# Two transformer blocks on one NeuronCore: both column blocks of a fresh LayerNorm's first unit in step, and a later spread of row scales

## The chip, the core and the metric

The kernel runs on one core of a Trainium2 chip. The metric is the device time of one execution in microseconds (us), from the runs' times; the profile adds one execution taken by the hardware profiler.

## What is computed

256 tokens of width 1024 go through two blocks of two layers each. In the first block every mixer and every MLP is followed by a LayerNorm of `DN_ALPHA * x + branch`; in the second each branch is `x + 0.5 * swiglu(rms_norm(x))` or a mixer. Cut to what the change touches:

```python
for i in range(DEPTH):                       # first block
    mix = attention_mixer(x, ...) if i % 2 == 0 else mamba2_bidir_mixer(x, ...)
    x = layer_norm(DN_ALPHA * x + mix, ln1_g[i], ln1_b[i])
    x = layer_norm(DN_ALPHA * x + squared_relu_mlp(x, mlp_w1[i], mlp_w2[i]), ln2_g[i], ln2_b[i])
...
def swiglu(h, w_gate, w_up, w_down):         # second block, begins with it
    return (jax.nn.silu(h @ w_gate) * (h @ w_up)) @ w_down
```

Everything is float32 in and out.

## The kernel before

The weights stream through the core in **units** of 1 MB: 1024 rows by 256 columns (eight chunks of 128 rows, two column blocks of 128), or 256 rows by 1024 columns for a down projection. A ring of three units lies in SBUF. SyncE loads a unit into `w_raw`; ScalarE casts it to the high half `w_hi` (L852, `split`); VectorE, or GpSimd for some stretches, subtracts to make the low half `w_lo` (L1383, L752) and signals `lo_ready`. TensorE takes a unit when its low half is there (`take`) and forms three products: high by high, low by high, high by low (`three`, L2078). `project_pair` (L2152 to L2156) does the same with operand halves joined into one matmul of 512 columns; its low products land in columns T to 2T of a PSUM bank and are added by ScalarE and VectorE when the bank is read. PSUM has eight banks of 512 float32 columns here: `pg` (four) and `acc` (four; they hold the running sums of the down projections).

Every engine runs its own program in the order in which the code is written; semaphores join them. There is no planner: what stands first in an engine's queue holds up what stands behind it.

**A fresh LayerNorm.** `ln` (VectorE, L1447 to L1456) makes the new `x` and its moments, ScalarE normalises the first 128 tokens (L889), VectorE the others in four parts (L1466). TensorE transposes the chunks into the `pg` banks (L2198), with a few matmuls on zeros in between (`warm`, L2310). ScalarE applies gain and bias, two chunks at a time, into `turn_buf` (L867); VectorE splits them into `op_hi` and `op_lo` (L1406, L1407 for chunks 0 and 1 one by one, L1412 and L1413 for each later pair) and signals `xt_ready`. The first unit that reads them, the fresh unit, waits at chunk 0, chunk 1 and the first chunk of each later pair:

```python
for c, k0, k1 in ((0, 0, 4), (1, 0, 4), (0, 4, 8), (1, 4, 8)) if halves else ((0, 0, 8), (1, 0, 8)):
    ...
        elif fresh and c == 0 and (k % 2 == 0 or fresh in LN_COUNT and k == 1):
            pe.wait_ge(xt_ready, TURN_BANK[fresh] + k // 2 + 1)
```

There are four such places: `ln1_0` (before the first MLP), `ln2_0` (before the SSM's input projection, through `project`), `ln1_1` (before the second MLP; behind the fresh unit TensorE computes a small product, L2664, and VectorE copies it to `rvec`, L1851, for which the first down projection waits on `rel_row`) and `ffn1_0` (the second block's first SwiGLU; the only one of the four with `halves`).

**A SwiGLU.** Unit 1 is a piece of the gate, unit 2 of the up projection, then units 3 (gate), 4 (up), 5 (down) and so on. The RMS norm is not applied to the operand; instead its row scale, one number for each token, multiplies the gate product. `spread_rstd` (TensorE, L2280) spreads the scales over all partitions into `acc` bank 1, ScalarE copies it (L987), and VectorE multiplies with it (L1516), after `gate_add`'s first step (L1512, signals `gate_taken`), which adds the low half that ScalarE copied out (L934). Behind this multiplication come, in the engines' order: ScalarE's silu (L939), ScalarE's cast of unit 4 (L852) and its copy of the up product (L945), VectorE's low half of unit 4 (L1383), and the sum of the up banks (L1521, signals `h_sum`), then the product (L1524), the hidden operand's high and low halves (L952, L1529, signals `h_ready`). TensorE waits for `gate_taken` before unit 3, for `h_sum` before unit 4, for `h_ready` before unit 5. In `ffn1_0` VectorE first finishes the LayerNorm's `x` (L1475, L1481), and ScalarE squares it for the scales (L918 to L923) and loads a function table (L1249) before it copies the gate product.

Of the kernel before, what the change touches and what calls it, by code (L numbers as in the profile page):

```python
# [11 lines left out]
ALU = mybir.AluOpType  # L12
AX = mybir.AxisListType

P = 128
T = 256
TT = T // P
D = 1024
KC = D // P
# [27 lines left out]
U = 256  # L47
# [47 lines left out]
LN_COUNT = {n: i + 1 for i, n in enumerate(LN_NAMES)}  # L95
NORM_AT = {n: sum(NORM_PARTS[:i]) for i, n in enumerate(TURNS)}
# [95 lines left out]
def two_blocks(nc, A, out):  # L192
    with ExitStack() as ctx:
# [229 lines left out]

        def oT_bank(a):

            return pg[:, 2 - 2 * a, :]

        def main_half(b):
            return pg[:, b:b + 2, 0:T]

        def low_half(b):
            return pg[:, b:b + 2, T:2 * T]
# [409 lines left out]
        def _(act):  # L842
# [88 lines left out]
            def gate_low(u_in, it=None, per_u=0):  # L931

                act.wait_ge(unit_done, at(u_in + 1, it, per_u))
                act.copy(act_pair, low_half(0)).then_inc(gate_lo, 1)  # L934
# [19 lines left out]
            def mlp(u0, h0, between=None, late=None):  # L954
                split(u0 + 2)
                hidden(h0, u0)
# [25 lines left out]
            def swiglu(u0, h0, ahead=False):  # L982
                if not ahead:
                    split(u0 + 2)
                gate_low(u0)
# [386 lines left out]
        def _(dve):  # L1372
# [137 lines left out]
            def gate_add(h, it=None, per_h=0, first=None):  # L1510
                dve.wait_ge(gate_lo, at(h - HG_FFN[0] + 1, it, per_h))
                dve.tensor_tensor(act_pair, main_half(0), act_pair, ALU.add).then_inc(gate_taken, 1)  # L1512
# [19 lines left out]
            def mlp(u0, h0, between=None):  # L1532
                split(u0 + 2)
                hidden(h0)
# [19 lines left out]
            def swiglu(u0, h0, ahead=False):  # L1554
                if not ahead:
                    split(u0 + 2)
                gate_add(h0, first=(h0 - HG_FFN[0]) // G2)
# [153 lines left out]
            for n in range(len(SSM_COLS)):  # L1711
# [29 lines left out]
                if n < CONV_UNITS:  # L1741
# [7 lines left out]
                    for k in order:  # L1749
                        for c in range(2):  # L1750
                            wc = COL["ssm_conv_w"] + 32 * k + (16 + 2 * i + c) % 32
                            t0, t1 = max(0, mid - k), T - max(0, k - mid)
                            src = pg[:, n % 4, c * T + t0 + k - mid:c * T + t1 + k - mid]
# [315 lines left out]
        def _(pe):  # L2069
# [15 lines left out]
            def feature_chunk(u, bank, c, step=U, fresh=None):  # L2085

                for k in range(KC):
                    if fresh and c == 0 and k and (k % 2 == 0 or fresh in LN_COUNT and k == 1):
                        pe.wait_ge(xt_ready, TURN_BANK[fresh] + k // 2 + 1)
# [13 lines left out]
            def project(u, bank, tokens=False, it=None, per=0, fresh=None):  # L2103
                take(u, it, per)
                if fresh in LN_COUNT:
                    pe.wait_ge(gained, TURN_BANK[fresh] + 1)
                    pe.wait_ge(half_ready, LN_COUNT[fresh])
                elif fresh:

                    pe.wait_ge(xt_ready, TURN_BANK[fresh] + 1)  # L2110
                for c in range(2):
                    o = bank[:, c * T:(c + 1) * T]
                    ins = token_tile(u, o, c, 0, U) if tokens else feature_chunk(u, o, c, fresh=fresh)
                ins.then_inc(unit_done, 1)
# [761 lines left out]
```

## Time and profile before

| | |
|---|---|
| median of 3 runs | 1729.44 us (1729.07 to 1729.72) |
| profiled execution | span 1727.7 us from its first to its last instruction; the page gives no other time for it |
| TensorE (PE) busy | 1700.7 us, 98% of the span, 9721 matmuls |
| TensorE weight loads (PEld) | 1458.1 us, beside the matmuls |
| VectorE (DVE) | 1175.8 us, 68% |
| ScalarE (ACT) | 922.0 us, 53% |
| GpSimd (POOL) | 297.4 us, 17% |
| DMA | 293.83 MB, 170 GB/s over the span |
| mean granted TensorE clock | 1.000 |

A row of a timeline gives the start of an instruction (or of a few alike), its duration, and in brackets how long its engine had been idle before it and which instruction ended that. Matmuls overlap, so the distance between two starts, not the duration, is what a matmul costs. A weight load (PEld) that starts behind a wait marks the same moment as its matmul.

### The profile page before, as it was taken

The numbers are of one execution on the slowest core, as the hardware profiler recorded it, in microseconds if no ns is written. First come the engines' busy times: TensorE is split into PE (matmuls) and PEld (weight loads), VectorE is DVE, ScalarE is ACT, GpSimd is POOL, SyncE is SP. The second block draws the span as 40 slices with busy tenths as digits, with TensorE's granted clock in tenths as the row PEclk, the third lists the DMA queues.
The fourth block names the chain that finished last, engine by engine and source line by source line (L and its number), as shares of the span: only waits on it lengthen the run. The fifth ranks groups of instructions, "written<-read, shape, count | busy, mean of one in ns | idle before, by whom it ended". The sixth has DMA issues, their size and how long they took to land.

```text
span 1727.7 us, 25216 instructions
## 1 busy us (share of the span) xinstructions
PE 1700.7 (98%) x9721; PEld 1458.1 (84%) x9721; DVE 1175.8 (68%) x1565; ACT 922.0 (53%) x1269; POOL 297.4 (17%) x162
## 2 busy tenths in 40 slices
PE   8999999999999999999999999999999999999999
PEld 8768888899888788878888978888888889878887
DVE  5887666778476875577666876666666667856665
ACT  4664444546674544465446566444554456664443
POOL 6003000675250130010000830000000006500000
PEclk9999999999999999999999999999999999999999
DMA  9425655556405575536564523665465554435652
GB/s 283 151 86 187 226 194 177 168 154 198 142 1 168 168 237 193 179 127 209 193 194 146 196 98 123 218 192 187 156 209 184 191 187 160 141 98 195 194 194 98
DMA packets 204268, 293.83 MB, mean 170 GB/s; under 512 B 6474, under 2 KB 169776, under 8 KB 204192
## 3 DMA queue, kind: packets, MB, share of 16 engines
q1 hardware_dynamic: 201072, 285.56, 50.6%
q0 software_dynamic: 2688, 6.47, 1.4%
q8 instruction: 52, 0.85, 0.2%
q10 hardware_dynamic: 432, 0.75, 0.1%
q14 instruction: 24, 0.20, 0.0%
HBM read 291.71 MB, written 1.05 MB: 169 GB/s over the span
## 4 chain that ended last, share of the span: by engine, by line
PE 89%; DVE 5%; ACT 4%; issue 1%; POOL 1%; DMA 0%; SPq 0%; ACTq 0%; DVEq 0%; POOLq 0%
PE acc L2078 30%; PE pg L2078 14%; PE pg L2152 13%; PE pg L2156 12%; PE pg L2155 6%; PE pg L2153 6%; PE acc L2616 1%; ACT w_hi L852 1%; PE pg L2603 1%; PE pg L2718 1%; ACT arena L1054 1%; PE pg L2198 1%; POOL w_lo L752 1%; ACT op L867 1%; DVE op L1421 1%
## 5 line engine op out<-in xcount | busy, mean ns | idle before, releaser
L1383 DVE TENSOR_TENSOR w_lo<-w_raw,w_hi 128x2048 fp32r<-128x2048 f32 x231 | 539.7, 2338 | 162.7 <-ACT w_hi L852 162.6
L852 ACT CAST w_hi<-w_raw 128x2048 fp32r<-128x2048 f32 x269 | 513.0, 1908 | 66.4 <-PE pg L2078 28.3
L2078 PE MATMUL acc<-w_hi,op 128*128 128x512 f32 x1600 | 517.5, 393 | 1.7 <-DVE op L2008 1.6
L2152 PE MATMUL pg<-op,w_hi 128*128 128x512 f32 x960 | 382.3, 398 | 7.0 <-DVE op L1413 1.9
L2156 PE MATMUL pg<-op,w_hi 128*128 128x512 f32 x960 | 379.7, 395 | 0.0
L2078 PEld LDWEIGHTS acc<-w_hi,op 128*128 128x128 f32 x1600 | 300.3, 188 | 66.9 <-issue 7.4
L2078 PE MATMUL acc<-w_lo,op 128*128 128x512 f32 x800 | 311.5, 389 | 0.0
L752 POOL TENSOR_TENSOR w_lo<-w_raw,w_hi 128x2048 fp32r<-128x2048 f32 x38 | 175.1, 4615 | 682.6 <-DVE w_lo L1383 630.2
L2155 PE MATMUL pg<-op,w_lo 128*128 128x256 f32 x960 | 267.6, 279 | 0.0
L2153 PE MATMUL pg<-op,w_lo 128*128 128x256 f32 x960 | 266.4, 277 | 0.0
L2078 PE MATMUL pg<-op,w_hi 128*128 128x256 f32 x1184 | 222.9, 287 | 2.9 <-DVE op L1421 1.2
L2155 PEld LDWEIGHTS pg<-op,w_lo 128*128 128x128 f32 x960 | 180.2, 188 | 44.3 <-DVE op L1407 0.9
L2153 PEld LDWEIGHTS pg<-op,w_lo 128*128 128x128 f32 x960 | 180.5, 188 | 39.7
L2152 PEld LDWEIGHTS pg<-op,w_hi 128*128 128x128 f32 x960 | 182.1, 190 | 16.9 <-issue 4.8
L2078 PEld LDWEIGHTS pg<-op,w_hi 128*128 128x128 f32 x1184 | 187.6, 192 | 7.3 <-issue 3.5
L2156 PEld LDWEIGHTS pg<-op,w_hi 128*128 128x128 f32 x960 | 179.9, 187 | 0.0
L2078 PEld LDWEIGHTS acc<-w_lo,op 128*128 128x128 f32 x800 | 150.3, 188 | 30.2
L2078 PE MATMUL pg<-op,w_lo 128*128 128x256 f32 x592 | 167.8, 283 | 0.0
L952 ACT CAST op<-h 128x512 fp32r<-128x512 f32 x76 | 47.2, 621 | 215.1 <-PE acc L2078 189.8
L1529 DVE TENSOR_TENSOR op<-h,op 128x512 fp32r<-128x512 f32 x76 | 57.0, 750 | 84.8 <-ACT op L952 84.8
L2078 PEld LDWEIGHTS pg<-op,w_lo 128*128 128x128 f32 x592 | 113.9, 192 | 0.5 <-issue 0.5
L934 ACT COPY act_buf<-pg 128x512 f32<-128x512 f32 x44 | 25.8, 586 | 115.1 <-PE pg L2156 115.0
(342 smaller groups left out, 1704.3 us busy)
## 6 DMA issues: line engine op xcount, KB each, us to landing
w_raw<-in_mlp_w SPq DMA_DIRECT2D x64, 1024.0 KB, 5.3
w_raw<-in_ffn_w_gate SPq DMA_DIRECT2D x44, 1024.0 KB, 5.3
w_raw<-in_ffn_w_up SPq DMA_DIRECT2D x44, 1024.0 KB, 5.3
w_raw<-in_ffn_w_down SPq DMA_DIRECT2D x44, 1024.0 KB, 4.8
w_raw<-in_ssm_w_in SPq DMA_DIRECT2D x24, 1024.0 KB, 5.3
w_raw<-in_w_in SPq DMA_DIRECT2D x20, 1024.0 KB, 5.1
w_raw<-in_attn_w_in SPq DMA_DIRECT2D x8, 1024.0 KB, 10.1
w_raw<-in_ssm_w_out SPq DMA_DIRECT2D x8, 1024.0 KB, 4.9
```

What stands on the lines that cost most here:

```text
L752: pool.tensor_tensor(w_lo[:, r, :], w_raw[:, r, :], w_hi[:, r, :].bitcast(F32), ALU.subtract) \
L852: act.copy(w_hi[:, u % RING, :], w_raw[:, u % RING, :]).then_inc(hi_ready, 1)
L867: ins = act.activation(op_hi[:, j, :] if bias is None else turn_buf[:, b % 2, c, :], turn_out(name, b)[:, c * T:(c + 1) * T], ACT.Identity ...
L934: act.copy(act_pair, low_half(0)).then_inc(gate_lo, 1)
L952: act.copy(op_hi[:, at_chunk:at_chunk + 2, :], h32[:, :].rearrange("p (c t) -> p c t", c=2)).then_inc(h_hi, 1)
L1383: dve.tensor_tensor(w_lo[:, s, :], w_raw[:, s, :], w_hi[:, s, :].bitcast(F32), ALU.subtract) \
L1529: dve.tensor_tensor(op_lo[:, dst, :], h32[:, :].rearrange("p (c t) -> p c t", c=2), op_hi[:, dst, :].bitcast(F32), ALU.subtract).then_inc( ...
L2078: ins = pe.matmul(psum, l, r, start=first and i == 0, stop=last and i == 2)
L2152: pe.matmul(bank, hi, joined, start=k == 0, stop=False)
L2153: pe.matmul(bank[:, 0:T], lo, op_hi[:, k, :], start=False, stop=False)
L2155: pe.matmul(bank[:, 0:T], lo, op_hi[:, k, :], start=False, stop=False)
L2156: ins = pe.matmul(bank, hi, joined, start=False, stop=k == KC - 1)
```

## The change

The fresh unit of the four LayerNorms takes the chunks in steps (0), (1), (2, 3), (4, 5), (6, 7), and each step for column block 0 and then for block 1. The waits stay where block 0 needs them. Block 1's bank can no longer be `pg` 1, which still holds transposed chunks at that time: `project_pair` writes the fresh unit to `acc` banks 2 and 3 (`FRESH`), and its readers (`hidden`, `gate_low`, `gate_add`) take it from there; in `ln2_0` block 0 stays in `pg` 0 and block 1 goes to `acc` bank 3, which the convolution reads. In `ffn1_0` the spread of the row scales moves from behind unit 2 to between the two column blocks of unit 3. Nothing is added or removed but this: the numbers and shapes of matmuls, casts and copies are the same.

```diff
+LN_STEPS = [(0, 1), (1, 2), (2, 4), (4, 6), (6, 8)]
...
+        def conv_src(n, c):
+            return acc[:, 3, 0:T] if n == 0 and c else pg[:, n % 4, c * T:(c + 1) * T]
...
+        FRESH = 4
+
+        def pair_banks(b):
+            return acc[:, 2:4, :] if b == FRESH else pg[:, b:b + 2, :]
+
         def main_half(b):
-            return pg[:, b:b + 2, 0:T]
+            return pair_banks(b)[:, :, 0:T]

         def low_half(b):
-            return pg[:, b:b + 2, T:2 * T]
+            return pair_banks(b)[:, :, T:2 * T]
...
             def mlp(u0, h0, between=None, late=None):
                 split(u0 + 2)
-                hidden(h0, u0)
+                hidden(h0, u0, b=FRESH)
...
-                gate_low(u0)
+                gate_low(u0, b=FRESH if ahead else 0)
                 act.wait_ge(rstd_spread, (h0 - HG_FFN[0]) // G2 + 1)
                 act.copy(token_rstd, acc[:, 1, 0:T]).then_inc(rb_ready, 1)
...
-                gate_add(h0, first=(h0 - HG_FFN[0]) // G2)
+                gate_add(h0, first=(h0 - HG_FFN[0]) // G2, b=FRESH if ahead else 0)
...
-                            src = pg[:, n % 4, c * T + t0 + k - mid:c * T + t1 + k - mid]
+                            src = conv_src(n, c)[:, t0 + k - mid:t1 + k - mid]
...
+            def project_fresh(u, fresh):
+
+                take(u)
+                for k0, k1 in LN_STEPS:
+                    for c in range(2):
+                        for k in range(k0, k1):
+                            if c == 0 and k == 0:
+                                pe.wait_ge(gained, TURN_BANK[fresh] + 1)
+                                pe.wait_ge(half_ready, LN_COUNT[fresh])
+                            elif c == 0 and (k == 1 or k % 2 == 0):
+                                pe.wait_ge(xt_ready, TURN_BANK[fresh] + k // 2 + 1)
+                            o = k * U + c * P
+                            ins = three(conv_src(0, c), wslice(u, o, o + P), (op_hi[:, k, :], op_lo[:, k, :]), k == 0,
+                                        k == KC - 1)
                 ins.then_inc(unit_done, 1)
...
             def project_pair(u, b, it=None, per=0, fresh=None, between=None, halves=False):
                 take(u, it, per)
-                for c, k0, k1 in ((0, 0, 4), (1, 0, 4), (0, 4, 8), (1, 4, 8)) if halves else ((0, 0, 8), (1, 0, 8)):
-                    bank = pg[:, b + c, :]
+                if fresh in LN_COUNT:
+                    order = [(c, k0, k1) for k0, k1 in LN_STEPS for c in range(2)]
+                else:
+                    order = ((0, 0, 4), (1, 0, 4), (0, 4, 8), (1, 4, 8)) if halves else ((0, 0, 8), (1, 0, 8))
+                for c, k0, k1 in order:
+                    bank = pair_banks(b)[:, c, :]
...
             def mlp(u0, h0, fresh, between=None, late=None):
-                project_pair(u0, 0, fresh=fresh)
+                project_pair(u0, FRESH, fresh=fresh)
...
             def swiglu(u0, h0, fresh, columns=None):
-                project_pair(u0, 0, fresh=fresh, halves=True,
+                project_pair(u0, FRESH if fresh in LN_COUNT else 0, fresh=fresh, halves=True,
                              between=(lambda: turn_half(fresh, 1)) if fresh in by_columns else None)
...
-                if fresh in LN_COUNT:
-                    project_pair(u0 + 1, 2)
-                    spread_rstd()
-                else:
-                    project_pair(u0 + 1, 2, between=spread_rstd)
+                late = fresh in LN_COUNT
+                project_pair(u0 + 1, 2, between=None if late else spread_rstd)

                 def group(u, h, it=None, first=False):

                     pe.wait_ge(gate_taken, at(h - HG_FFN[0], it, 1))
-                    project_pair(u, 0, it, 3)
+                    project_pair(u, 0, it, 3, between=spread_rstd if first and late else None)

                     pe.wait_ge(h_sum, at(h, it, 1))
                     project_pair(u + 1, 2, it, 3)
...
+                elif n == 0:
+                    project_fresh(u, "ln2_0")
                 else:
-                    project(u, bank, fresh="ln2_0" if n == 0 else None)
+                    project(u, bank)
```

TensorE's order in the fresh unit of `ln1_0`, before (line numbers of the kernel before; `half_ready`, `gained` and `xt_ready` are the operand's signals):

```order
L2152 MATMUL pg<-op,w_hi 128x512 [waits half_ready,gained,lo_ready]
L2153 MATMUL pg<-op,w_lo 128x256
L2155 MATMUL pg<-op,w_lo 128x256 [waits xt_ready]
L2156 MATMUL pg<-op,w_hi 128x512
L2152 MATMUL pg<-op,w_hi 128x512 [waits xt_ready]
L2153 MATMUL pg<-op,w_lo 128x256
L2155 MATMUL pg<-op,w_lo 128x256
L2156 MATMUL pg<-op,w_hi 128x512
L2152 MATMUL pg<-op,w_hi 128x512 [waits xt_ready]
L2153 MATMUL pg<-op,w_lo 128x256
```

and now (line 2173 is the old 2152, 2174 the old 2153, 2176 and 2177 the old 2155 and 2156):

```order
L2173 MATMUL acc<-op,w_hi 128x512 [waits half_ready,gained,lo_ready]
L2174 MATMUL acc<-op,w_lo 128x256
L2173 MATMUL acc<-op,w_hi 128x512
L2174 MATMUL acc<-op,w_lo 128x256
L2176 MATMUL acc<-op,w_lo 128x256 [waits xt_ready]
L2177 MATMUL acc<-op,w_hi 128x512
L2176 MATMUL acc<-op,w_lo 128x256
L2177 MATMUL acc<-op,w_hi 128x512
L2173 MATMUL acc<-op,w_hi 128x512 [waits xt_ready]
L2174 MATMUL acc<-op,w_lo 128x256
```

The first chunk's two matmuls and the second chunk's two now stand twice, once for each block, before the third chunk's wait; before, block 1 stood behind all eight chunks of block 0.

TensorE's order in `ffn1_0` from the end of unit 2, before:

```order
L2155 MATMUL pg<-op,w_lo 128x256
L2156 MATMUL pg<-op,w_hi 128x512
L2280 MATMUL acc<-ident,rstd 128x128 [waits rstd_ready]
L2280 MATMUL acc<-ident,rstd 128x128
L2152 MATMUL pg<-op,w_hi 128x512 [waits lo_ready,gate_taken]
L2153 MATMUL pg<-op,w_lo 128x256
```

now at the same place:

```order
L2174 MATMUL pg<-op,w_lo 128x256
L2176 MATMUL pg<-op,w_lo 128x256
L2177 MATMUL pg<-op,w_hi 128x512
L2173 MATMUL pg<-op,w_hi 128x512 [waits lo_ready,gate_taken]
L2174 MATMUL pg<-op,w_lo 128x256
```

and between the two blocks of unit 3 (line 2301 is the old 2280):

```order
L2176 MATMUL pg<-op,w_lo 128x256
L2177 MATMUL pg<-op,w_hi 128x512
L2301 MATMUL acc<-ident,rstd 128x128 [waits rstd_ready]
L2301 MATMUL acc<-ident,rstd 128x128
L2173 MATMUL pg<-op,w_hi 128x512
L2174 MATMUL pg<-op,w_lo 128x256
```

The spread stood ahead of the wait for `gate_taken`; it now stands sixteen matmuls behind it. On ScalarE and VectorE only the names of the banks that are read change, not the order.

## Rows read from the trace of the kernel before

**Rows 1.** The profile's page: shares of the last chain; GpSimd's subtractions.

```profile
PE 89%; DVE 5%; ACT 4%; issue 1%; POOL 1%; DMA 0%; SPq 0%; ACTq 0%; DVEq 0%; POOLq 0%
...
L752 POOL TENSOR_TENSOR w_lo<-w_raw,w_hi 128x2048 fp32r<-128x2048 f32 x38 | 175.1, 4615 | 682.6 <-DVE w_lo L1383 630.2
```

**Rows 2.** Timeline of PE, ln1_0: start us, us, instruction, [idle before <-releaser].

```profile
127.44 0.50 PE L2152 MATMUL pg<-op,w_hi 128*128 128x512 f32 x1 [0.50 <-DVE op L1413]
...
129.75 0.50 PE L2152 MATMUL pg<-op,w_hi 128*128 128x512 f32 x1
...
130.55 0.40 PE L2152 MATMUL pg<-op,w_hi 128*128 128x512 f32 x1
...
133.34 0.40 PE L2152 MATMUL pg<-op,w_hi 128*128 128x512 f32 x1
```

**Rows 3.** Timeline of all engines, ln1_0: VectorE behind the fresh unit.

```profile
129.61 4.48 DVE L1383 TENSOR_TENSOR w_lo<-w_raw,w_hi 128x2048 fp32r<-128x2048 f32 x2
...
136.26 0.69 DVE L1529 TENSOR_TENSOR op<-h,op 128x512 fp32r<-128x512 f32 x1 [0.69 <-ACT op L952]
```

**Rows 4.** Timeline of all engines, ln2_0: TensorE (PE, PEld) and VectorE.

```profile
310.71 0.39 PE L2078 MATMUL pg<-op,w_hi 128*128 128x256 f32 x1 [0.49 <-DVE op L1413]
...
312.88 2.28 DVE L1383 TENSOR_TENSOR w_lo<-w_raw,w_hi 128x2048 fp32r<-128x2048 f32 x1
313.01 0.19 PEld L2078 LDWEIGHTS pg<-op,w_hi 128*128 128x128 f32 x1 [0.33 <-DVE op L1413]
...
316.58 0.40 PE L2078 MATMUL pg<-op,w_hi 128*128 128x256 f32 x2
```

**Rows 5.** Timeline of all engines, ln1_1; the last row from PE's own.

```profile
569.90 0.50 PE L2152 MATMUL pg<-op,w_hi 128*128 128x512 f32 x1 [0.45 <-DVE op L1413]
...
572.06 4.49 DVE L1383 TENSOR_TENSOR w_lo<-w_raw,w_hi 128x2048 fp32r<-128x2048 f32 x2
...
575.88 0.81 PE L2664 MATMUL acc<-arena 32*4 32x384 f32 x2
...
580.11 0.54 DVE L1851 COPY arena<-acc 4x384 f32<-4x384 f32 x1
...
582.31 0.39 PE L2078 MATMUL acc<-w_hi,op 128*128 128x512 f32 x1
```

**Rows 6.** Timeline of PE, ffn1_0.

```profile
767.28 0.69 PE L2280 MATMUL acc<-ident,rstd 128*128 128x128 f32 x4
768.94 0.50 PE L2152 MATMUL pg<-op,w_hi 128*128 128x512 f32 x1 [0.98 <-DVE act_buf L1512]
...
771.85 0.39 PE L2152 MATMUL pg<-op,w_hi 128*128 128x512 f32 x1
...
775.06 0.50 PE L2152 MATMUL pg<-op,w_hi 128*128 128x512 f32 x1 [0.26 <-DVE h L1521]
```

**Rows 7.** Timelines of ACT and of DVE, ffn1_0.

```profile
768.06 0.38 ACT L987 COPY xn<-acc 128x256 f32<-128x256 f32 x1
...
768.92 0.69 DVE L1516 TENSOR_TENSOR act_buf<-act_buf,xn 128x512 f32<-128x512 f32 x1
...
774.32 0.68 DVE L1521 TENSOR_TENSOR h<-pg,h 128x512 f32<-128x512 f32 x1
```

**Rows 8.** Timelines of PE, ACT and DVE in the SwiGLU at 1065 us.

```profile
1065.07 0.61 PE L2280 MATMUL acc<-ident,rstd 128*128 128x128 f32 x4
...
1065.72 0.37 ACT L987 COPY xn<-acc 128x256 f32<-128x256 f32 x1 [2.76 <-PE acc L2280]
...
1066.19 0.69 DVE L1516 TENSOR_TENSOR act_buf<-act_buf,xn 128x512 f32<-128x512 f32 x1 [0.81 <-ACT xn L987]
```

**Rows 9.** Timeline of PE, the start of the kernel.

```profile
7.72 2.34 PE L2198 MATMUL pg<-ident,X 128*128 128x128 f32 x10
...
10.70 0.42 PE L2078 MATMUL pg<-op,w_lo 128*128 128x256 f32 x1
...
12.55 0.28 PE L2078 MATMUL pg<-op,w_lo 128*128 128x256 f32 x1
```

More of the change, by code:

```diff
@@ L929, in hidden, with gate_low @@
                 act.copy(act_pair, low_half(b)).then_inc(act_done, 1)
-            def gate_low(u_in, it=None, per_u=0):
+            def gate_low(u_in, it=None, per_u=0, b=0):
                 act.wait_ge(unit_done, at(u_in + 1, it, per_u))
-                act.copy(act_pair, low_half(0)).then_inc(gate_lo, 1)
+                act.copy(act_pair, low_half(b)).then_inc(gate_lo, 1)
             def gate_silu(h, it=None, per_h=0):
@@ L1508, in hidden, with gate_add @@
                                          op1=ALU.mult).then_inc(h32_ready, 1)
-            def gate_add(h, it=None, per_h=0, first=None):
+            def gate_add(h, it=None, per_h=0, first=None, b=0):
                 dve.wait_ge(gate_lo, at(h - HG_FFN[0] + 1, it, per_h))
-                dve.tensor_tensor(act_pair, main_half(0), act_pair, ALU.add).then_inc(gate_taken, 1)
+                dve.tensor_tensor(act_pair, main_half(b), act_pair, ALU.add).then_inc(gate_taken, 1)
                 dve.wait_ge(gate_taken, at(h - HG_FFN[0] + 1, it, per_h))
@@ L1533, in mlp @@
                 split(u0 + 2)
-                hidden(h0)
+                hidden(h0, b=FRESH)
                 hidden_lo(h0)
@@ L2083, in wslice, with feature_chunk @@
                 return w_hi[:, s, a:z], w_lo[:, s, a:z]
-            def feature_chunk(u, bank, c, step=U, fresh=None):
+            def feature_chunk(u, bank, c, step=U):
                 for k in range(KC):
-                    if fresh and c == 0 and k and (k % 2 == 0 or fresh in LN_COUNT and k == 1):
-                        pe.wait_ge(xt_ready, TURN_BANK[fresh] + k // 2 + 1)
                     o = k * step + c * P
@@ L2101, in token_tile, with project @@
                 return ins
-            def project(u, bank, tokens=False, it=None, per=0, fresh=None):
-                take(u, it, per)
-                if fresh in LN_COUNT:
[L2106 to L2110, printed above, removed]
-                for c in range(2):
-                    o = bank[:, c * T:(c + 1) * T]
-                    ins = token_tile(u, o, c, 0, U) if tokens else feature_chunk(u, o, c, fresh=fresh)
+            def project(u, bank):
+                take(u)
+                for c in range(2):
+                    ins = feature_chunk(u, bank[:, c * T:(c + 1) * T], c)
+                ins.then_inc(unit_done, 1)
+            def project_fresh(u, fresh):
+                take(u)
+                for k0, k1 in LN_STEPS:
[9 more added lines that the diff above has]
+                                        k == KC - 1)
                 ins.then_inc(unit_done, 1)
@@ L2282, in spread_rstd @@
                     ins.then_inc(rstd_spread, 1)
-                if fresh in LN_COUNT:
-                    project_pair(u0 + 1, 2)
-                    spread_rstd()
-                else:
-                    project_pair(u0 + 1, 2, between=spread_rstd)
+                late = fresh in LN_COUNT
+                project_pair(u0 + 1, 2, between=None if late else spread_rstd)
                 def group(u, h, it=None, first=False):
                     pe.wait_ge(gate_taken, at(h - HG_FFN[0], it, 1))
-                    project_pair(u, 0, it, 3)
+                    project_pair(u, 0, it, 3, between=spread_rstd if first and late else None)
                     pe.wait_ge(h_sum, at(h, it, 1))
```

## The prediction

> **What bounds the kernel now.** The chain of work that ended last comes first: TensorE holds nearly nine tenths of it [rows 1], so a microsecond counts only where it is idle time of TensorE, or work of another engine that TensorE waits for. The list of waits led me to the places where it idles, and the timelines there show both: a few tenths of a microsecond at a time behind VectorE's conversion of a fresh LayerNorm (L1413) [rows 2], and once 0.98 us behind L1512 in the first SwiGLU [rows 6]. The place at 755 to 776 us needs a second reading: there the chain runs through ScalarE and VectorE.
>
> I call the four places by their LayerNorms: ln1_0 (125 us), ln2_0 (309 us), ln1_1 (568 us), ffn1_0 (755 us). "Fresh" is the unit that reads the LayerNorm; the one behind it is "the next".
>
> **ln1_0.** Before, column block 0 goes through all eight chunks and waits for each pair, then block 1 runs without a wait. The second pair starts at 127.44, the fourth at 129.75, block 1 at 130.55, the next unit at 133.34 [rows 2]. So two chunks of one block take (133.34 - 130.55) / 4 = 0.70 us, and 0.10 more behind a wait (130.55 - 129.75 = 0.80). After, chunks 0 and 1 of block 1 (0.35 us each) fill the waits ahead of 127.44, and each later pair is 1.40 us of work, while the operands come one pair in (129.75 - 127.44) / 2 = 1.16 us. So only the second pair still waits. It ends at 127.44 + 1.50 = 128.94, the third at 130.34, later than the fourth is ready, the fourth at 131.74. That is 133.34 - 131.74 = 1.60 us.
>
> What is late next is the next unit's low half. VectorE begins it at 129.61, two such subtractions in 4.48 us [rows 3], so it ends at about 131.87; with 0.05 for a start TensorE goes on at 131.9. Saved: 1.4 us. Does it last? The next unit now ends at 131.9 + 5.6 = 137.5. The down projection behind it needs the hidden low half, L1529, done at 136.26 + 0.69 = 136.95 [rows 3]; VectorE's queue (the two subtractions, which do not depend on the fresh unit) sets that time, so it stays. 0.5 us of slack: it lasts.
>
> **ln2_0.** Same form, with three matmuls of 256 columns for a chunk of one block. Before, the last pair starts at 313.01 and ten such threes follow; the next unit's first matmul is the second of the row at 316.58, at 316.70 [rows 4]. That is 0.36 us each and 0.1 for the start. After, the second pair starts at 310.71 and twelve threes follow: 310.71 + 0.1 + 4.3 = 315.1. The next unit's low half ends at 312.88 + 2.28 = 315.16 [rows 4]. TensorE goes on at 315.2: 1.5 us. Behind it GpSimd's subtractions take 4.6 us each [rows 1] against 16 threes, 5.8 us, so it does not become the bound.
>
> **ln1_1.** After: 569.90 + 1.50 + 1.40 + 1.40 = 574.2 for the end of the fresh unit. The small matmul L2664 began at 575.88 [rows 5] and now begins at 574.3, when the low half is ready too (572.06 + 2.25). Saved: 1.6 us. The output unit, at 582.31 before, comes at 580.7; VectorE's L1851, for which it waits, ends at 580.11 + 0.54 = 580.65 [rows 5]. Covered by a hair: each tenth that L1851 slips goes back, up to the 1.6 us.
>
> **ffn1_0, the interleaving.** Here four chunks of each block already alternate. Both ways only the second pair waits long enough to matter; what is gained is the 0.7 us of block 1's first two chunks, now ahead of it. With the spread (L2280) moved away, TensorE reaches its wait for gate_taken at 767.28 - 0.7 = 766.6. But the wait's end, 768.94, is set by L1512, behind ScalarE's copy L934 [rows 6], which stands behind two squares, roots and a table load of the RMS norm. None of these depends on the fresh unit. The third unit still starts at 768.94. I cost this part at nothing: the idle time only grows from 1.0 to 2.3 us.
>
> **ffn1_0, the spread.** Before, it started at 767.28 and ScalarE copied it at 768.06, hidden under L1512; the scaling L1516 came at 768.92 directly behind it [rows 6, 7]. Queued behind L1516, in order: ScalarE's silu, its high-half cast, VectorE's low half, then L1521 at 774.32, which frees the up banks. TensorE's fourth unit waited for L1521 and started at 775.06 [rows 6, 7]. After, the spread stands between the two blocks of the third unit. Nothing moves that unit's start, so the spread starts where block 1 started, 771.85 [rows 6]. From spread to copy takes 0.65 us, from copy to scaling 0.47 where nothing else holds them: 1065.07, 1065.72, 1066.19 in a later SwiGLU [rows 8]. From scaling to L1521 it is 774.32 - 768.92 = 5.40, and to TensorE 0.74 more. Sum: 771.85 + 0.65 + 0.47 + 5.40 + 0.74 = 779.1, against 775.06: **4.0 us later**. The third unit with the spread ends near 775.3, so TensorE idles some 3.8 us. Behind it the casts, the low halves and the output unit are queued behind the same steps and shift with them; from 775.06 on TensorE was continuous, so nothing gives it back. In the other three SwiGLUs the spread is in the second unit, one unit earlier, and the 5.6 us of that unit cover the chain; that place stays.
>
> **The clock.** The profile shows no comparable stop: TensorE's longest behind the start is about 1 us. At the start, where TensorE had done nothing before the transposes at 7.72, matmuls of 256 columns took 0.42 us (10.70) and from 12.55 on 0.28 [rows 9]: 1.2 GHz first and 2.4 GHz later, though the granted clock reads 1.00 there. That is a slow stretch of up to 4.8 us; half of it, 2.4 us, is what it would cost here if the 3.8 us of idle brought the lower level back. The bounds of this unknown are 0 and 2.4 us. I take 0: the nearest row is the stop of 0.98 us, behind which eight chunks took 771.85 - 768.94 = 2.91 us [rows 6], the 0.70 for two and the start. The Trainium skill (TensorE: Matmul & The Clock Gate, "Why this matters for your kernels") speaks against the change: it wants no long idle between bursts, since the array then falls to half rate. By that rule the sum would be the second rival's, by the row of 0.98 us the forecast's.
>
> **Sum.** -1.4 - 1.5 - 1.6 + 4.0 = -0.5 us. The profiled execution spans 1727.7 us; the runs have a median of 1729.44, which is 1.7 us around the span, and I leave that as it is: **1728.9 us**. About 0.2%, 3.5 us, is what a measurement of this kernel tells from no change, so the forecast is "same", with its own range of 1728 to 1730.
>
> **Rivals.**
> 1. *The gains stay out and the spread's cost comes* (slower). Mechanism: in ln1_0 and ln2_0 TensorE arrives at the next low half just as it ends, and in ln1_1 at L1851 within 0.1 us; if TensorE's earlier arrival only turns into waits there, the 4.0 us stand alone: 1729.4 + 4.0 = 1733.4. It decides from the point where the three gains together fall below 0.5 us. For it: three covers under 0.5 us. Against: VectorE's queue does not wait for the fresh unit, so the rows give ends, not durations. Chance 0.11.
> 2. *The clock falls in ffn1_0*: -0.5 + 2.4 = +1.9, 1731.3; up to 1733 if two stretches are slow. For it: 6 us of idle in 12.5. Against: no row of such a fall after the start. Chance 0.24.
> 3. *The spread's delay is absorbed* (the change does its work and no more): 1729.4 - 4.5 = 1724.9, or 1727 if half is. For it: ScalarE and VectorE idle later in the SwiGLU. Against: L1521 stands behind the scaling in both queues by their order. Chance 0.11.
> The forecast has 0.54.
>
> **Numbers.** Range 1726.5 to 1733.0: the forecast, all of the clock's case and the halves of the other two; about 0.15 lies outside. Faster by over 0.2% (below 1726.0): most of the third rival, 0.08. Slower (above 1732.9): the first rival and a tail of the second, 0.14. Same: 0.78.
>
> **What would show it.** In ln1_0, ln2_0 and ln1_1 only the waits ahead of the second pair remain, and the next unit starts 1.4, 1.4 and 1.6 us sooner after the fresh unit's start. In ffn1_0 the spread (L2301 in the new numbering) starts about 3 us into the third unit, and TensorE shows an idle of 3 to 4 us released by the sum of the up banks. If that idle is under 1 us, the main term is wrong; if 512-column matmuls behind it stand 0.43 instead of 0.23 us apart, the clock's rival is right; if new waits for a low half appear in the first three places, the first rival.

## The result and the profile after

The median is **1731.99 us** (21 runs, 1730.55 to 1733.94) against 1729.77 us for the kernel before (21 runs, 1729.07 to 1730.12): a ratio of 1.0014, with 95% interval 1.0008 to 1.002. So the change costs 2.2 us, where I forecast 0.5 us less. 1731.99 lies in the stated range, but at the second rival's 1731.3 and on the wrong side of the starting time. The scatter has also grown, from 1.1 to 3.4 us, and the time follows the mean granted clock of TensorE: the six executions with 0.999 took 1730.55 to 1731.04 us, the nine with 0.998 took 1731.46 to 1732.72, the six with 0.997 took 1733.52 to 1733.94. The profiled execution took 1733.58 us around its span of 1731.5, so it lies at the upper end of the runs.

The page of the kernel after: span, busy time of each engine, and the shares of the chain that ended last. That chain has less TensorE in it than before [rows 1].

```profile
span 1731.5 us, 25208 instructions
...
PE 1701.6 (98%) x9713; PEld 1460.9 (84%) x9721; DVE 1175.7 (68%) x1565; ACT 922.2 (53%) x1269; POOL 295.2 (17%) x162
...
PE 87%; DVE 5%; ACT 4%; issue 1%; DMA 1%; POOL 1%; SPq 0%; ACTq 0%; DVEq 0%; POOLq 0%
```

Two of TensorE's waits after, from the list of waits (in total, times, longest). The 3.9 us one is the largest behind the start. The 1.8 us at three places are the wait for the fresh unit's first chunk (L1417, the old L1407), and they are as long as before: the change doesn't touch them.

```profile
PE pg L2173 <- DVE h L1531: 3.9, 1, 3.9
...
PE acc L2173 <- DVE op L1417: 1.8, 3, 0.7
```

What the interleaving aims at is the wait for the later pairs. In the list before it stands as below, with 0.7 us more at two places of L2078; the list after has no such line (L1413 is L1423 now).

```profile
PE pg L2152 <- DVE op L1413: 1.9, 5, 0.5
```

The three places ahead of the SwiGLU, in TensorE's timeline (start us, us, instruction). Of ln1_0 you see the first chunk, the second pair and the next unit, of ln2_0 the first chunk and the next unit, of ln1_1 the first chunk and the small matmul L2684, and last the start of ffn1_0's fresh unit.

```profile
125.86 0.47 PE L2173 MATMUL acc<-op,w_hi 128*128 128x512 f32 x1 [0.56 <-DVE op L1417]
...
127.54 0.50 PE L2173 MATMUL acc<-op,w_hi 128*128 128x512 f32 x1
...
132.04 0.50 PE L2173 MATMUL pg<-op,w_hi 128*128 128x512 f32 x1
...
307.84 0.36 PE L2088 MATMUL pg<-op,w_hi 128*128 128x256 f32 x1
...
314.03 0.39 PE L2088 MATMUL pg<-op,w_hi 128*128 128x256 f32 x1
...
565.63 0.47 PE L2173 MATMUL acc<-op,w_hi 128*128 128x512 f32 x1 [0.66 <-DVE op L1417]
...
571.65 0.81 PE L2684 MATMUL acc<-arena 32*4 32x384 f32 x2
...
750.79 0.47 PE L2173 MATMUL acc<-op,w_hi 128*128 128x512 f32 x1 [0.57 <-DVE op L1417]
```

The fresh unit of ln1_0 starts 0.10 us later than before, that of ln2_0 1.20 sooner (309.04 before), that of ln1_1 2.63 sooner (568.26), that of ffn1_0 4.26 sooner (755.05). The differences are what each place gave: 1.30, 1.43 and 1.63 us, **4.36 us together**, and all of it is kept until 750.79.

It goes in the 39 us behind: the unit at 790.17 starts 3.91 us later than before (786.26), and the spans differ by about as much. TensorE's timeline in ffn1_0, from the third unit on:

```profile
764.69 0.50 PE L2173 MATMUL pg<-op,w_hi 128*128 128x512 f32 x1 [2.19 <-DVE act_buf L1522]
...
767.11 0.63 PE L2173 MATMUL pg<-op,w_hi 128*128 128x512 f32 x1
...
768.39 0.46 PE L2173 MATMUL pg<-op,w_hi 128*128 128x512 f32 x1
...
769.16 0.61 PE L2301 MATMUL acc<-ident,rstd 128*128 128x128 f32 x4
...
776.41 0.80 PE L2173 MATMUL pg<-op,w_hi 128*128 128x512 f32 x1 [3.85 <-DVE h L1531]
...
777.43 0.63 PE L2177 MATMUL pg<-op,w_hi 128*128 128x512 f32 x1
777.86 0.63 PE L2173 MATMUL pg<-op,w_hi 128*128 128x512 f32 x1
778.29 0.41 PE L2174 MATMUL pg<-op,w_lo 128*128 128x256 f32 x1
...
779.14 0.63 PE L2173 MATMUL pg<-op,w_hi 128*128 128x512 f32 x1
...
782.62 0.39 PE L2173 MATMUL pg<-op,w_hi 128*128 128x512 f32 x1
```

Three things are to be seen. First, the fourth unit starts at 776.41, behind an idle time of 3.85 us that ends with L1531. It was 20.01 us behind the start of the fresh unit before (775.06 - 755.05) and is 25.62 behind it now. Second, the rows of the third unit's block 0: 767.11 to 768.39 is 1.28 us for two chunks, where 0.70 is normal, so the block takes 769.16 - 764.69 = 4.47 us instead of the 2.91 of [rows 6]: +1.56 us. Third, the same in the fourth unit: 777.86 to 779.14 is 1.28 us; from 782.62 on two chunks take 0.70 again (the next rows of this form stand at 783.31 and 784.01). From 776.41 to 782.62 five pairs of chunks took 6.21 us, 2.6 more than five normal ones with a start. The 5.61 us that the fourth unit lost are 1.56 of the first slow stretch and 4.05 of the moved step. Worked out by itself, the step gives the same: 2.91 us to the spread and 7.25 from there to the fourth unit (next view), against 775.06 - 768.94 = 6.12 before, is 4.04.

The chain behind the spread, in the timelines of ScalarE and VectorE:

```profile
769.80 0.37 ACT L997 COPY xn<-acc 128x256 f32<-128x256 f32 x1 [5.89 <-PE acc L2301]
771.01 0.63 ACT L949 ACTIVATE act_buf<-act_buf 128x512 f32<-128x512 f32 x1 [0.83 <-DVE act_buf L1526]
771.54 1.89 ACT L862 CAST w_hi<-w_raw 128x2048 fp32r<-128x2048 f32 x1
...
770.28 0.69 DVE L1526 TENSOR_TENSOR act_buf<-act_buf,xn 128x512 f32<-128x512 f32 x1 [5.64 <-ACT xn L997]
773.46 2.29 DVE L1393 TENSOR_TENSOR w_lo<-w_raw,w_hi 128x2048 fp32r<-128x2048 f32 x1 [2.49 <-ACT w_hi L862]
775.67 0.68 DVE L1531 TENSOR_TENSOR h<-pg,h 128x512 f32<-128x512 f32 x1
```

It is the one that I had priced: spread at 769.16, copy at 769.80, scaling at 770.28, then silu, cast and low half, L1531 at 775.67, TensorE at 776.41. That is 7.25 us (7.26 forecast).

The windows of ffn1_0 (stretch, then its length, and busy time with the number of instructions of PE, PEld, DVE, ACT and POOL; then PEclk, the granted clock, then the DMA's share and its GB/s):

```profile
765.00:767.00 2.00, 2.00 (x8) 1.77 (x7) 0.00 (x0) 0.00 (x0) 0.00 (x0) 0.52 1.08 383
767.00:769.00 2.00, 2.00 (x9) 1.66 (x9) 0.00 (x0) 0.00 (x0) 0.00 (x0) 0.62 0.12 33
...
776.00:778.00 2.00, 1.59 (x5) 1.40 (x6) 1.21 (x3) 0.81 (x2) 0.00 (x0) 0.50 0.50 95
...
782.00:784.00 2.00, 2.00 (x12) 1.70 (x12) 1.97 (x3) 0.63 (x1) 0.00 (x0) 0.96 0.29 37
```

The third unit runs its first part at a granted 0.52 to 0.62, the fourth at 0.50, which is TensorE's 1.2 GHz in place of 2.4, up to about 782; ahead of the first fall TensorE was idle for 2.19 us, ahead of the second for 3.85. The account of the profiled execution: -4.36 + 4.05 + 1.56 + 2.6 = +3.85; the spans differ by 1731.5 - 1727.7 = 3.8.

### The profile page after: what moved, and what is told of

Same layout as the page of the kernel before. It is cut to its first block, busy times and chain, and to the rows that moved or that the text cites. A ratio compares the mean times of both kernels' runs of the same rounds, so it can differ in the third digit from the quotient of the medians.

```text
span 1731.5 us, 25208 instructions
## 1 busy us (share of the span) xinstructions
PE 1701.6 (98%) x9713; PEld 1460.9 (84%) x9721; DVE 1175.7 (68%) x1565; ACT 922.2 (53%) x1269; POOL 295.2 (17%) x162
## 4 chain that ended last, share of the span: by engine, by line
PE 87%; DVE 5%; ACT 4%; issue 1%; DMA 1%; POOL 1%; SPq 0%; ACTq 0%; DVEq 0%; POOLq 0%
PE acc L2088 30%; PE pg L2173 13%; PE pg L2177 12%; PE pg L2088 12%; PE pg L2176 6%; PE pg L2174 6%; PE acc L2636 1%; DVE w_lo L1393 1%; ACT w_hi L862 1%; DMA w_raw<-in_attn_w_in 1%; PE pg L2623 1%; ACT op L877 1%; PE pg L2738 1%; PE pg L2219 1%; ACT arena L1064 1%
## 5 line engine op out<-in xcount | busy, mean ns | idle before, releaser
L2173 PE MATMUL pg<-op,w_hi 128*128 128x512 f32 x936 | 373.7, 399 | 7.9 <-DVE h L1531 3.9
L2177 PE MATMUL pg<-op,w_hi 128*128 128x512 f32 x936 | 371.8, 397 | 0.0
L2176 PE MATMUL pg<-op,w_lo 128*128 128x256 f32 x936 | 261.6, 279 | 0.0
L2174 PE MATMUL pg<-op,w_lo 128*128 128x256 f32 x936 | 260.6, 278 | 0.0
L2088 PE MATMUL pg<-op,w_hi 128*128 128x256 f32 x1168 | 219.1, 286 | 2.2 <-DVE op L1431 1.2
L2176 PEld LDWEIGHTS pg<-op,w_lo 128*128 128x128 f32 x936 | 176.7, 189 | 42.8
L2174 PEld LDWEIGHTS pg<-op,w_lo 128*128 128x128 f32 x936 | 177.1, 189 | 39.4
L2173 PEld LDWEIGHTS pg<-op,w_hi 128*128 128x128 f32 x936 | 178.7, 191 | 15.4 <-DVE h L1531 4.2
L2088 PEld LDWEIGHTS pg<-op,w_hi 128*128 128x128 f32 x1168 | 184.6, 192 | 6.8 <-issue 3.2
L2177 PEld LDWEIGHTS pg<-op,w_hi 128*128 128x128 f32 x936 | 176.4, 188 | 0.0
L2088 PE MATMUL pg<-op,w_lo 128*128 128x256 f32 x584 | 165.2, 283 | 0.0
L2088 PEld LDWEIGHTS pg<-op,w_lo 128*128 128x128 f32 x584 | 112.1, 192 | 0.3 <-issue 0.2
```

The costliest lines, as they stand in the source:

```text
L2088: ins = pe.matmul(psum, l, r, start=first and i == 0, stop=last and i == 2)
L2173: pe.matmul(bank, hi, joined, start=k == 0, stop=False)
L2174: pe.matmul(bank[:, 0:T], lo, op_hi[:, k, :], start=False, stop=False)
L2176: pe.matmul(bank[:, 0:T], lo, op_hi[:, k, :], start=False, stop=False)
L2177: ins = pe.matmul(bank, hi, joined, start=False, stop=k == KC - 1)
```

## The experiments

Each was timed beside the kernel before, whose median was 1729.84 us beside experiments 1 to 4, 1729.71 beside 5 to 8 and 1729.79 beside 9 and 10. Single executions lie 5 to 6 us above the others of their kernel, with a mean granted clock of 0.996 to 0.999: four of 67 of the kernel before (1735.6 to 1735.8), two of 11 in experiment 1, one of 12 in each of 6, 7 and 8; no profile holds one, so their cause is open. Diffs are against the kernel after, unless said otherwise. "Unit 3" and "unit 4" are the third and fourth unit of ffn1_0.

**1. The spread back to its old place.** It separates the two parts of the change.

```diff
-                late = fresh in LN_COUNT
-                project_pair(u0 + 1, 2, between=None if late else spread_rstd)
+                if fresh in LN_COUNT:
+                    project_pair(u0 + 1, 2)
+                    spread_rstd()
+                else:
+                    project_pair(u0 + 1, 2, between=spread_rstd)
...
-                    project_pair(u, 0, it, 3, between=spread_rstd if first and late else None)
+                    project_pair(u, 0, it, 3)
```

> The change with the spread of the row scales back behind unit 2 of ffn1_0; the interleaving stays. Theory A (the late spread holds up the chain to the sum of the up banks by 4.0 us, and the idle time it leaves lets the clock fall, 1 to 4.6 us more): the three gains of 1.3, 1.4 and 1.6 us remain alone, 1725.4 us, ratio 0.9975, with runs as close together as before's. Theory B (the interleaving itself costs in ffn1_0, because TensorE arrives sooner and idles 2.2 us before unit 3, enough for the clock to fall): 1727 to 1729 us, with runs scattered.

Measured: 1725.63 us (nine executions at 1725.21 to 1726.20, two at 1730.7), ratio 0.9982 (0.9973 to 0.9991); the medians alone give 0.9976. TensorE's timeline:

```profile
762.79 0.71 PE L2301 MATMUL acc<-ident,rstd 128*128 128x128 f32 x4 [0.50 <-DVE down_scale L1508]
764.48 0.50 PE L2173 MATMUL pg<-op,w_hi 128*128 128x512 f32 x1 [0.97 <-DVE act_buf L1522]
...
770.60 0.50 PE L2173 MATMUL pg<-op,w_hi 128*128 128x512 f32 x1 [0.26 <-DVE h L1531]
```

The gain of the interleaving stands alone, 4.2 us, and the waits of unit 3 and unit 4 are those of [rows 6], 0.97 and 0.26 us. So the late spread with all that it brings costs 1731.99 - 1725.63 = 6.4 us.

**2. The late spread alone,** in the kernel before, without the interleaving.

```diff
-                if fresh in LN_COUNT:
-                    project_pair(u0 + 1, 2)
-                    spread_rstd()
-                else:
-                    project_pair(u0 + 1, 2, between=spread_rstd)
+                late = fresh in LN_COUNT
+                project_pair(u0 + 1, 2, between=None if late else spread_rstd)
...
-                    project_pair(u, 0, it, 3)
+                    project_pair(u, 0, it, 3, between=spread_rstd if first and late else None)
```

> The kernel before with the spread moved between the two blocks of unit 3 in ffn1_0, and nothing else. Theory A: unit 4 starts 4.0 us later, and the clock falls in the idle time: 1733.8 us without a fall, up to 1738 with one, runs scattered over some 3 us. Theory B: 1733.8 us at most, since the idle time before unit 3 is only 1.6 us here, with little scatter; if the late spread were free, 1729.8.

Measured: 1735.64 us (five executions, 1735.50 to 1737.28), ratio 1.0035 (1.0022 to 1.0049): +5.8 us. TensorE's timeline, and two windows of 5 us:

```profile
769.40 0.50 PE L2152 MATMUL pg<-op,w_hi 128*128 128x512 f32 x1 [1.49 <-DVE act_buf L1512]
...
779.54 0.50 PE L2152 MATMUL pg<-op,w_hi 128*128 128x512 f32 x1 [3.84 <-DVE h L1521]
...
769.00:774.00 5.00, 4.60 (x28) 4.12 (x29) 0.94 (x2) 0.37 (x1) 0.00 (x0) 1.00 0.62 202
779.00:784.00 5.00, 4.46 (x17) 3.84 (x17) 3.10 (x4) 3.69 (x4) 0.00 (x0) 0.66 0.64 210
```

Unit 3 waits 1.49 us and runs at full speed behind it; the only fall is the one behind the 3.84 us, a granted 0.66 in 779 to 784. 4.05 us for the step leaves 1.8 us for this fall.

**3. The kernel after, with both idle times filled** by matmuls on zeros: 7 ahead of unit 3, 14 ahead of unit 4. The order of the real work stays, and if the rest of the loss is the clock, only the 4.0 us remain.

```diff
+                    if first and late:
+                        warm(acc[:, 0, :], 7)
                     pe.wait_ge(gate_taken, at(h - HG_FFN[0], it, 1))
...
+                    if first and late:
+                        warm(acc[:, 0, :], 14)
                     pe.wait_ge(h_sum, at(h, it, 1))
```

> The change with 7 matmuls on zeros before the wait for gate_taken and 14 before the wait for h_sum, in ffn1_0's first group alone, so that TensorE is not idle there. Theory A: the clock stays up, the 4.0 us of the chain stay: 1729.8 - 4.3 + 4.0 = 1729.5 us (up to 0.5 more where the matmuls on zeros overhang), with little scatter. If the clock alone were the cost: 1725.4. If the clock has no part: 1732.0 as the change.

Measured: 1729.55 us (1729.09 to 1729.94), ratio 0.9998 (0.9989 to 1.0007). TensorE's timeline, with the zeros at 771.28, and the window behind unit 4's start:

```profile
771.28 3.23 PE L2332 MATMUL acc<-zeros 128*128 128x512 bf16 x13
775.27 0.50 PE L2173 MATMUL pg<-op,w_hi 128*128 128x512 f32 x1 [0.76 <-DVE h L1531]
...
775.00:779.00 4.00, 3.73 (x21) 3.28 (x22) 2.09 (x4) 2.95 (x4) 0.00 (x0) 1.00 0.73 246
```

More work on the engine that bounds the kernel makes it 2.4 us faster than the kernel after, and the scatter falls from 3.4 to 0.9 us. Unit 4 still starts where the chain lets it, 775.27 - 765.12 = 10.15 us behind unit 3, the 2.91 + 7.25 of before; the zeros themselves hold nothing up, and the delay is a cost by itself: 1729.55 - 1725.63 = 3.9 us. What the filling gave back, **1731.99 - 1729.55 = 2.4 us**, is the clock.

**4. The spread ahead of unit 3,** directly behind the wait for gate_taken.

```diff
+                    if first and late:
+                        spread_rstd()
-                    project_pair(u, 0, it, 3, between=spread_rstd if first and late else None)
+                    project_pair(u, 0, it, 3)
```

> The change with the spread directly behind the wait for gate_taken and ahead of unit 3's first block: a half dose of the delay. Theory A: the scaling comes 1.12 us behind that point, the sum of the up banks 5.4 us later, so unit 4 starts 7.3 us behind the wait's end, where the spread and unit 3 take 6.3: a wait of 1.0 us, no fall of the clock of its own, 1725.4 + 1.2 = 1726.6 us. Theory B: as the run with the spread back, plus 0.7.

Measured: 1726.61 us (1726.25 to 1727.25), ratio 0.9977 (0.9968 to 0.9986). TensorE's timeline and a window:

```profile
765.07 0.71 PE L2301 MATMUL acc<-ident,rstd 128*128 128x128 f32 x4 [2.18 <-DVE act_buf L1522]
...
772.42 0.50 PE L2173 MATMUL pg<-op,w_hi 128*128 128x512 f32 x1 [1.06 <-DVE h L1531]
...
763.00:769.00 6.00, 3.93 (x24) 3.54 (x25) 1.68 (x4) 3.60 (x6) 0.00 (x0) 1.00 0.55 178
```

Three microseconds sooner in TensorE's queue, and the wait of unit 4 is 1.06 us in place of 3.85. The 2.18 us of idle ahead are as long as in the kernel after, and this time no fall of the clock follows.

**5. Experiment 1, with ScalarE's cast for unit 4 ahead of the silu.** It tests whether the last 0.26 us ahead of unit 4 is the queue's order as well.

```diff
+                if ahead:
+                    split(u0 + 3)
                 gate_silu(h0)
-                split(u0 + 3)
+                if not ahead:
+                    split(u0 + 3)
```

> The change with the spread back behind unit 2, and ScalarE's cast of unit 4 ahead of the silu in ffn1_0's first group. If the wait of 0.26 us before unit 4 hangs on the order spread, scaling, silu, cast, low half, it goes: 1725.6 - 0.26 = 1725.4 us. If something else sets it, 1725.6.

Measured: 1724.8 us (1724.36 to 1725.0), ratio 0.9969 (0.9957 to 0.998). The wait is gone, and the gain over experiment 1, 0.8 us, or 0.7 with each taken against the kernel before beside it, is larger than expected. The traces show that a wait of 0.26 us costs more than 0.26: from the last pair of chunks of unit 3 to the second pair of unit 4 it is 771.41 - 769.47 = 1.94 us in experiment 1 and 770.61 - 769.21 = 1.40 here, a difference of 0.54 us.

**6 and 7. One idle time filled at a time,** to see which of them brings the fall. Experiment 6 has only the first of experiment 3's two insertions (7, ahead of the wait for gate_taken), experiment 7 only the second:

```diff
+                    if first and late:
+                        warm(acc[:, 0, :], 14)
                     pe.wait_ge(h_sum, at(h, it, 1))
```

> The change with 7 matmuls on zeros before the wait for gate_taken alone; the idle time of 3.9 us before unit 4 stays empty. If both idle times lower the clock by themselves, only the second fall is left: 1729.55 + 1.8 = 1731.3 us, scatter under 1.5 us. If the falls come from the first idle time and last: 1729.6.

> The change with 14 matmuls on zeros before the wait for h_sum alone; the idle time of 2.2 us before unit 3 stays empty. If both idle times lower the clock by themselves, the first fall comes in some executions, costing 0 to 1.6 us: 1729.5 to 1731.2 us, median 1730.2. If only the longer idle time counts: 1729.6 with the scatter of before.

Measured for 6: 1731.73 us (1730.47 to 1732.42, a wider scatter than expected, and one at 1738.05), ratio 1.001 (0.9999 to 1.002). TensorE's timeline, and the windows of unit 3 and of unit 4's first part:

```profile
764.84 0.50 PE L2173 MATMUL pg<-op,w_hi 128*128 128x512 f32 x1 [0.65 <-DVE act_buf L1522]
...
774.98 0.50 PE L2173 MATMUL pg<-op,w_hi 128*128 128x512 f32 x1 [3.84 <-DVE h L1531]
...
763.00:769.00 6.00, 5.35 (x31) 4.06 (x30) 0.94 (x3) 1.39 (x4) 0.00 (x0) 1.00 0.56 178
...
775.00:779.00 4.00, 4.00 (x16) 3.48 (x17) 2.18 (x3) 3.24 (x4) 0.00 (x0) 0.67 0.80 260
```

Measured for 7: 1730.31 us, ratio 1.0003 (0.9995 to 1.0012), its executions in two groups, six at 1729.46 to 1729.82 with a mean granted clock of 1.000 and five at 1730.79 to 1731.45 with 0.999, and one at 1735.67. The same views:

```profile
764.97 0.50 PE L2173 MATMUL pg<-op,w_hi 128*128 128x512 f32 x1 [2.20 <-DVE act_buf L1522]
...
776.70 0.50 PE L2173 MATMUL pg<-op,w_hi 128*128 128x512 f32 x1 [0.77 <-DVE h L1531]
...
763.00:769.00 6.00, 4.03 (x16) 3.52 (x17) 0.89 (x3) 1.15 (x3) 0.00 (x0) 0.77 0.59 178
...
775.00:779.00 4.00, 3.23 (x18) 2.24 (x16) 3.03 (x4) 1.53 (x2) 0.00 (x0) 1.00 0.42 109
```

Each filling removes the fall behind it and leaves the other. The long idle time alone costs 1731.73 - 1729.55 = 2.2 us, the short one alone 1730.31 - 1729.55 = 0.8 us in the median. The two groups of experiment 7 and their clocks fit a short idle time that is sometimes followed by a fall that costs some 1.5 us and sometimes by none; its one profile, of the 1731.45 us execution, is of the first sort. Together they are 3.0 us against the 2.4 of experiment 3, which the scatter of the kernel after, 3.4 us, does not let me tell apart.

**8. ffn1_0 as before, the interleaving in the other three places only.**

```diff
-                if fresh in LN_COUNT:
+                if fresh in LN_COUNT and not halves:
...
-                project_pair(u0, FRESH if fresh in LN_COUNT else 0, fresh=fresh, halves=True,
+                project_pair(u0, 0, fresh=fresh, halves=True,
```

With it go the old bank for the readers (`gate_low`, `gate_add`) and the edit of experiment 1.

> The interleaving in ln1_0, ln2_0 and ln1_1 alone; ffn1_0 is the kernel before's, order, banks and spread. If the interleaving in ffn1_0 is worth nothing, as costed: 1725.6 us, the same as the run with the spread back. If it brings its 0.7 us: 1726.3. If it costs (TensorE idle longer before unit 3): 1725.2 or less.

Measured: 1725.45 us (1724.96 to 1726.02, and one at 1731.53), ratio 0.9976 (0.9967 to 0.9984), the same as experiment 1. The interleaving in ffn1_0 is worth nothing there: TensorE merely arrives sooner at a wait whose end another chain sets.

**9. The late spread kept, and the work behind it let past.** If the 4.0 us come from what is queued behind the spread's consumers, reordering ScalarE and VectorE must remove them and both idle times. ScalarE copies the gate's low part between the two RMS tiles and does the cast for unit 4 and the copy of the up banks before it waits for the spread; VectorE adds the gate halves ahead of unit 3's low half and does unit 4's low half before the scaling.

```diff
             def swiglu(u0, h0, ahead=False):
                 if not ahead:
                     split(u0 + 2)
-                gate_low(u0, b=FRESH if ahead else 0)
+                    gate_low(u0)
+                else:
+                    split(u0 + 3)
+                    up_low(h0, u0 + 1)
                 act.wait_ge(rstd_spread, (h0 - HG_FFN[0]) // G2 + 1)
...
                     rms_tile(0, x_final, 0)
+                    gate_low(U_FFN[0], b=FRESH)
                     rms_tile(1, x_final, 0)
...
-                gate_add(h0, first=(h0 - HG_FFN[0]) // G2, b=FRESH if ahead else 0)
-                split(u0 + 3)
+                if ahead:
+                    split(u0 + 3)
+                    gate_scaled(h0, first=(h0 - HG_FFN[0]) // G2)
...
+                    dve.wait_ge(gate_lo, 1)
+                    dve.tensor_tensor(act_pair, main_half(FRESH), act_pair, ALU.add).then_inc(gate_taken, 1)
                     split(U_FFN[0] + 2)
```

> The change with its late spread, and the queues of ffn1_0's first group reordered: ScalarE copies the gate's low half between the two RMS tiles, casts unit 4 and copies the up's low half before it waits for the spread; VectorE adds the gate's halves before unit 3's low half, and makes unit 4's low half before the scaling. If the late spread costs only through what is queued behind it, nothing that TensorE waits for hangs on it now: unit 3 starts 1.3 us sooner and unit 4 1.1 us sooner than with the spread back, 1725.6 - 1.1 = 1724.5 us, no fall of the clock. If the late spread costs by itself: 1729 or more.

Measured: **1723.61 us** (1723.45 to 1724.13), ratio 0.9966 (0.9952 to 0.9979). TensorE's timeline, and the windows of 763 to 775:

```profile
762.87 0.47 PE L2187 MATMUL pg<-op,w_hi 128*128 128x512 f32 x1 [0.72 <-DVE w_lo L1398]
...
765.73 0.60 PE L2315 MATMUL acc<-ident,rstd 128*128 128x128 f32 x4
...
763.00:769.00 6.00, 6.00 (x37) 5.30 (x38) 4.15 (x5) 3.37 (x4) 0.00 (x0) 1.00 0.64 190
769.00:775.00 6.00, 6.00 (x36) 5.21 (x34) 4.16 (x5) 4.73 (x4) 0.00 (x0) 1.00 0.47 162
```

The spread still stands inside unit 3, no wait of unit 4 is left, the idle time ahead of unit 3 is 0.72 us in place of 2.19 and ends with another instruction, the low half (L1398), and TensorE is busy for all of these 12 us at a granted 1.00. This version beats both kernels, and the expectation by 0.9 us. Part of that is in ffn1_0: from the start of the fresh unit to the start of the unit behind unit 5 it takes 779.98 - 750.45 = 29.53 us, against 781.82 - 750.58 = 31.24 in experiment 1, a gain of 1.7 us where 1.1 were expected.

**10. The same reordering, spread back to its old place** (the edits of experiments 1 and 9 together).

```diff
-                gate_low(u0, b=FRESH if ahead else 0)
+                    gate_low(u0)
+                else:
+                    split(u0 + 3)
+                    up_low(h0, u0 + 1)
...
+                if fresh in LN_COUNT:
+                    project_pair(u0 + 1, 2)
+                    spread_rstd()
```

> The same reordering with the spread back behind unit 2. TensorE then waits there for the scales, ready 0.7 us later than before for the added step in VectorE's queue: unit 3 starts at the scales plus 0.7 us, about 1 us later than in the run with the late spread, unit 4 behind it without a wait: 1724.9 us. If the place of the spread is indifferent now: 1724.5.

Measured: 1724.22 us (1723.86 to 1724.45), ratio 0.9968 (0.9956 to 0.998). Now the early spread is the worse one, by 0.6 us; in its profile it waits 1.09 us in TensorE's queue for VectorE's L1513 (down_scale). With the independent work let past, the late place costs nothing against the early one: the 3.9 us of the kernel after came from what is queued behind the spread's consumers.

## Why the prediction missed

**ln1_0, ln2_0, ln1_1: held.** 1.30, 1.43 and 1.63 us against 1.4, 1.5 and 1.6; inside the places it reads the same: the next unit of ln1_0 starts 132.04 - 125.86 = 6.18 us behind the fresh one (7.58 before), and L2684 in ln1_1 571.65 - 565.63 = 6.02 us (7.62 before). The waits ahead of the second pair, which were to remain, are too short for the list. The first rival, that these gains turn into new waits, is out: experiments 1 and 8 keep 4.2 to 4.3 us of the forecast 4.5. The thin cover of ln1_1 held: L1861 (the old L1851) ends at 577.33 + 0.54 = 577.87, and the output unit starts at 578.08, 12.45 us behind the fresh one (14.05 before).

**The interleaving in ffn1_0: held** at nothing (experiment 8 against 1); the idle time grew to 2.19 us, as worked out.

**The late spread: held.** 4.0 us forecast; 4.05 in the profile, 3.9 between experiments 1 and 3. The idle time ahead of unit 4 is 3.85 us, as worked out; the spread starts 4.47 us into the third unit and not 3, since that unit ran at the lower clock. The third rival, that the delay is absorbed, is out for this order of the queues; experiment 9 shows the order with which it becomes true.

**The clock: this step failed.** "The bounds of this unknown are 0 and 2.4 us. I take 0: the nearest row is the stop of 0.98 us". The price of 0 was the failed term: it was 2.4 us in the median (the kernel after against experiment 3), and the forecast of a small gain turned into a loss. The mechanism was in the text as the second rival, with its price; what was wrong was the value taken between the bounds. I took the nearest row, a stop of 0.98 us, for one of 2.2 and one of 3.8 us, although it is far shorter than either, and that the page showed no fall behind short stops says nothing of long ones. The sign named for that rival is there too: 777.43 to 777.86 is 0.43 us between two matmuls of 512 columns. The Trainium skill (TensorE: Matmul & The Clock Gate, "Why this matters for your kernels") spoke for the fall, and the traces agree: a granted 0.50 behind 3.85 us of idle. They also show a fall behind 2.19 us, shorter than the gaps that the page warns of. With 2.4 the sum is 1731.3, within 0.7 us of the result; 0.3 of the 0.7 is the starting time (1729.77 us in 21 runs, 1729.44 in the three that I started from), and some 0.3 the gains, 4.2 in place of 4.5. That the upper bound equals the median loss is luck. It was half of one slow stretch at the kernel's start, and that stretch was read from a row that the view had cut off at its left edge: the transposes begin at 6.42 and not at 7.72, so up to 6.1 us are slow, and the same working gives 3.1. What was measured is two stretches of changing size, 2.2 us behind the long idle time alone, 0.8 behind the short one alone, and 1.56 + 2.6 = 4.2 us together in the profiled execution.

```profile
6.42 3.65 PE L2198 MATMUL pg<-ident,X 128*128 128x128 f32 x16 [6.42 <-DMA X<-in_x]
```

**The range and the chances.** The forecast took 3.5 us as the least change that can be told from none. That was too coarse: the interval of the ratio, 1.0008 to 1.002, excludes no change at +2.2 us. 1733.0 as upper end covered the median but not the upper executions, up to 1733.94. In the profiled one both falls occur, and experiment 1's 1725.63 with 3.9 and 4.2 makes 1733.7, where the six upper ones lie. "Up to 1733 if two stretches are slow" was the right picture, given too little weight.

## What to carry to other kernels

A step is priced by what is queued behind its consumers: moving one half-microsecond of TensorE work by a few microseconds cost 4 us here, and letting the independent work past made the same place harmless. Before you open an idle time of 2 to 4 us, as here, on a busy TensorE, add the clock to its price, and where it can't be closed, fill it with matmuls on zeros and see whether time and scatter fall. When an added idle time has no comparable row in the profile, don't carry over the price of a shorter one.

## What the runs showed of the hardware

- Idle times of TensorE of 0.97 us (experiment 1) and 1.49 us (experiment 2) left the granted clock at 1.00. Those of 3.84 and 3.85 us (the kernel after, experiments 2 and 6) were followed by the lower level in every profile taken. Those of 2.18 to 2.20 us were followed by it in two profiles (the kernel after and experiment 7) and not in a third (experiment 4). What decides in that case stays open; no run here shows it.
- The cost differs from one execution to the next: the kernel after lies at 1730.55 to 1733.94 while its mean granted clock reads 0.999 to 0.997, and the kernel with filled idle times spreads over 0.9 us. A scatter that grows with a change is a sign to look at the clock, not a proof: the kernel before has single executions near 1735.7 us too (mean granted clock 0.998), which no profile explains.
- At the lower level a pair of chunks took 1.28 us in place of 0.70, a factor of 1.83 and not 2 (the kernel after, ffn1_0).
- A wait costs TensorE more than its listed idle time: the 0.26 us ahead of unit 4 in experiment 1 cost 0.54 us between the starts of matmuls, against experiment 5.
- At the start of the kernel matmuls of 256 columns took 0.42 us [rows 9] while the granted clock reads 1.00; the same form took 0.41 us (778.29, the kernel after) beside a granted 0.50, and 0.28 at full speed. So look at the durations too, and not at that column alone.
